# A decoder layer with a gathered expert stage: the on-chip row ring moved to a multiple of 8,192 bytes

## The chip, the cores and the metric

One core of a Trainium2 chip runs the whole kernel. The metric is the device time of one execution, in microseconds: the median of three runs is 3116.35 us (3115.84 to 3116.93). All arithmetic is in float32.

## The reference, cut to what matters

The layer normalises 1,040 tokens (16 meta tokens and 1,024 inputs), projects them, runs differential attention beside a gated causal convolution, projects the two back and adds the residual. Then comes the expert stage, with which this change has to do. For each of 1,024 tokens, and for each of 8 heads, it takes a query, scores it against two sets of 128 keys, keeps the 16 best pairs, and so names 16 of 16,384 experts:

```
q = (xt @ wq).reshape(PEER_CHUNK, PEER_HEADS, 2, PEER_HALF)
s = jnp.einsum('thpk,hpnk->thpn', q, subkeys)
...
e = i1 * PEER_KEYS + i2
gate = jax.nn.softmax(c_top, axis=-1)
act = jax.nn.gelu(jnp.einsum('thkd,td->thk', u_tab[e], xt), approximate=False)
w = (gate * act)
return jnp.einsum('thk,thkd->td', w, v_tab[e])
```

Every token thus needs 128 rows of u and 128 rows of v, each of 1,024 floats. A last norm follows. `x` is (1, 1024, 1024), `peer_u` and `peer_v` are (1, 16384, 1024), `peer_wq` is (1, 1024, 2048).

## The kernel before, in words

The program has two phases, one after the other, each in a block of its own. `mixer_phase` does the norm, the input projection, the convolution and the attention of the first four tiles of 128 tokens. `expert_phase` does the experts of all eight tiles, and beside them the output projection of all tiles and the attention of the last four.

In the expert phase a step is one tile and one head: 64 steps, of 16 experts each, so 1,024 gathers in all. The table in device memory has one row for each expert, u beside v: 2,048 floats, 8,192 bytes. Gather g (`pool.indirect_dma_start`, L1040) brings 128 such rows, one to a partition, and puts them into slot g mod 8 of `ring`, a tensor of 8 slots of 8,192 bytes in each partition. GpSimd issues it when slot g mod 8 is free (`b_free`) and, at the first of a step, when the step's expert numbers are there (`b_route`).

What then happens to gather g, in order: VectorE multiplies the first half of the slot with the normalised tokens `xn_even` or `xn_odd` and sums (`dot`, L1426); ScalarE takes the gelu (L1258), multiplies with the gate (L1184) and makes a diagonal matrix of it (L1191); TensorE multiplies the second half of the slot with this diagonal in 8 matmuls of 64 x 64 x 512 and adds into `acc` (`combine`, L1623). The last of them frees the slot. Between these, written out by hand in the loops over m and k, stand the routing of the steps m + 1 and m + 2 (`queries` at L1597, with weights from `wq_first` for head 0 and `wq_rest` for the others; the top-16 search on VectorE, which uses `top_v`, `top_i`, `cand`, `c_top`, `c_idx`, `c_ab`, `hot` and `pick`), the late attention, the projection and the norms. SyncE issues all other transfers of the phase; they run on the same 16 DMA engines as the gathers.

On-chip memory is given out in the order in which the tensors are named: each begins where the last one ended, its size in a partition rounded up to 32 bytes. The tensors of the mixer phase are given back before those of the expert phase are placed, and the expert phase begins at byte 74,944 of each partition. In the built program of the kernel before, `wq_first` stands at 57,472, `wq_rest` at 75,072, `g2_row` at 132,416, `ring` at 138,560, `xn_even` at 204,096, `xn_odd` at 208,192; in the mixer phase `xT`, which has 8 rows of 4,160 bytes, stands at 81,792.

Of the kernel before, what the change touches and what calls it, by code (L numbers as in the profile page):

```python
# [7 lines left out]
U32 = mybir.dt.uint32  # L8
# [6 lines left out]
P = 128  # L15
D = 1024
# [18 lines left out]
TOPK = 16  # L35
QH = 128
CAND = TOPK * TOPK
RING = 8
# [812 lines left out]
def expert_phase(nc, shared, x, g2, wq, w_out, table, g_final, out, dram):  # L851

    ctx = ExitStack()
    with ctx:
        def sb(name, shape, dt=F32):
            return ctx.enter_context(nc.sbuf_tensor(name, shape, dt))
# [8 lines left out]
        wide, keys_s, wq_first = shared["wide"], shared["keys"], shared["wq0"]  # L865
        mix_t, h_next, proj = shared["mix"], shared["h"], shared["proj"]
        w_out_s = wide[:].rearrange("p (k n) -> p k n", k=KC)
        iota_i = sb("iota_i", [P, TOPK], I32)
        iota_f = sb("iota_f", [P, TOPK])
        wq_rest = sb("wq_rest", [P, PH - 1, KC, 2 * QH])  # L870
        g2_row = sb("g2_row", [P, D])
        gf_half = sb("gf_half", [P, 512])
        ring = sb("ring", [P, RING, 2 * D])
        xn = [sb("xn_even", [P, D]), sb("xn_odd", [P, D])]
        xnT = sb("xnT_cur", [P, KC, P])
        nrm = sb("nrm", [P, 2])
        fin = sb("fin", [P, 2, 2])
        q_s = sb("q_s", [P, 2 * QH])
        qT_s = sb("qT_s", [P, 2, P])
        top_v = sb("top_v", [P, 2, TOPK])  # L880
        top_i = sb("top_i", [P, 2, TOPK], U32)
        cand = sb("cand", [P, CAND])
        cand_t = sb("cand_t", [P, CAND])
        c_top = sb("c_top", [P, TOPK])
        c_idx = sb("c_idx", [P, TOPK], U32)
        c_ab = sb("c_ab", [P, 2, TOPK], U32)
        hot = sb("hot", [P, 2 * TOPK, TOPK])
        pick = sb("pick", [P, 2, TOPK])
        neg_top = sb("neg_top", [P, 1])
        g_exp = sb("g_exp", [P, TOPK])  # L890
        g_sum = sb("g_sum", [P, 2])
        e_row = [sb("e_even", [P, TOPK], U32), sb("e_odd", [P, TOPK], U32)]
        gate = [sb("gate_even", [P, TOPK]), sb("gate_odd", [P, TOPK])]
# [861 lines left out]
def program(nc, x, xt, w_units, w_v, lam_vecs, params, w_out, g2, wq, subkeys_t, table, g_final, out):  # L1755
# [13 lines left out]
    with ExitStack() as ctx:  # L1769

        shared = {
            "wide": ctx.enter_context(nc.sbuf_tensor("wide", [P, KC * D], F32)),
            "keys": ctx.enter_context(nc.sbuf_tensor("keys_s", [P, PH * 2, KEYS], F32)),
            "wq0": ctx.enter_context(nc.sbuf_tensor("wq_first", [P, KC, 2 * QH], F32)),
            "mix": ctx.enter_context(nc.sbuf_tensor("mix_t", [P, KC, P], F32)),
            "h": ctx.enter_context(nc.sbuf_tensor("h_next", [P, D], F32)),
            "ident": ctx.enter_context(nc.sbuf_tensor("ident", [P, P], F32)),
            "pairs": ctx.enter_context(nc.sbuf_tensor("pairs", [P, 2, HP], F32)),
            "sub_gain": ctx.enter_context(nc.sbuf_tensor("sub_gain", [P, 1], F32)),
            "lam": ctx.enter_context(nc.sbuf_tensor("lam_s", [P, 4], F32)),  # L1780
            "proj": [ctx.enter_context(nc.psum_tensor(f"proj{b}", [P, 512], F32)) for b in range(2)],
            "h_in": ctx.enter_context(nc.semaphore("h_in")),
            "w_out_in": ctx.enter_context(nc.semaphore("w_out_in")),
            "keys_in": ctx.enter_context(nc.semaphore("keys_in")),
            "wq0_in": ctx.enter_context(nc.semaphore("wq0_in")),
        }
        mixer_phase(nc, shared, x, xt, w_units, w_v, lam_vecs, params, w_out, wq, subkeys_t, dram)
        expert_phase(nc, shared, x, g2, wq, w_out, table, g_final, out, dram)
# [34 lines left out]
```

## Time and profile before

| | |
|---|---|
| median of three runs | 3116.35 us |
| the profiled execution | 3116.56 us |
| its span, first to last instruction | 3114.8 us |
| mean granted TensorE clock | 0.857 of full speed |
| PE, DVE, ACT, POOL busy | 74%, 67%, 43%, 38% |
| read from device memory, written | 1122.06 MB, 15.28 MB |
| the gathers' queue (q0) | 84.1% of the 16 DMA engines' span |

PE is TensorE, DVE VectorE, ACT ScalarE, POOL GpSimd, SP SyncE, PEld the weight load of TensorE. The busy shares are means over the whole span, and the mixer phase (the first 415 us) looks quite unlike the expert phase. Shares of the DMA engines can go a little over 100%, because the profile lets a packet begin about when the one before it is still ending.

### The profile page before, as it was taken

The page shows a single profiled execution, that of the slowest core. Times are in us where ns is not written, and L with a number is a line of the kernel's source. Part 1 is how long each engine was busy: PE and PEld are TensorE (multiplying, and loading weights), DVE is VectorE, ACT ScalarE, POOL GpSimd, SP SyncE. Part 2 cuts the span into 40 slices and gives each one's busy share as a digit, 9 for nine tenths or more (in the row PEclk, how much of TensorE's full clock was granted, in tenths as well). Part 3 has the DMA queues.
Part 4 walks back from the last instruction along what each step waited for, and adds up shares of the span by engine and source line. Part 5 has one row for each costly group of instructions (what it writes and reads, how often), then busy time and mean ns, then how long its engine had stood idle before and what let it go on. Part 6 is the DMA issues. An engine that isn't in the chain of part 4 may idle for free.

```text
span 3114.8 us, 35490 instructions
## 1 busy us (share of the span) xinstructions
PE 2304.2 (74%) x11776; PEld 846.1 (27%) x11776; DVE 2071.9 (67%) x4903; ACT 1330.3 (43%) x3979; POOL 1176.2 (38%) x1077
## 2 busy tenths in 40 slices
PE   9998847777777777677676777677767777777775
PEld 5555522222222222232222222222222222222111
DVE  2997426666677777777666666666666666666664
ACT  1023514444355555554544444444444444444433
POOL 1001004444444444454444444444444444433442
PEclk9999979898789888999888888978888788887776
DMA  5002139999999999999999999999999999999997
GB/s 213 21 27 72 59 147 420 421 420 421 420 415 410 421 414 411 417 415 419 408 417 421 421 421 421 420 421 416 418 420 417 421 417 419 416 422 418 418 413 312
DMA packets 165608, 1139.68 MB, mean 366 GB/s; under 512 B 18608, under 2 KB 21040, under 8 KB 32688
## 3 DMA queue, kind: packets, MB, share of 16 engines
q0 software_dynamic: 150096, 1082.80, 84.1%
q1 hardware_dynamic: 15328, 54.62, 4.6%
q8 instruction: 93, 1.52, 0.2%
q14 instruction: 91, 0.75, 0.1%
HBM read 1122.06 MB, written 15.28 MB: 365 GB/s over the span
## 4 chain that ended last, share of the span: by engine, by line
DMA 47%; PE 19%; ACT 10%; DVE 6%; issue 4%; POOL 0%; SPq 0%; DVEq 0%; POOLq 0%; ACTq 0%
DMA ring<-table,e_odd 25%; DMA ring<-table,e_even 20%; PE acc L1623 11%; DVE ring L1426 5%; PE qq_ps L1597 4%; ACT diag L1191 2%; ACT weight L1184 2%; ACT L1258 1%; ACT L1177 1%; ACT gelu L1258 1%; PE proj L1570 1%; ACT wide L1215 1%; PE acc L1661 1%; DVE wide L1441 1%; DMA mix_dram<-mix_t 1%
## 5 line engine op out<-in xcount | busy, mean ns | idle before, releaser
L1623 PE MATMUL acc<-ring,diag 64*64 64x512 f32 x8192 | 1330.7, 735 | 729.0 <-ACT diag L1191 704.8
L1426 DVE CUSTOM_DVE_ANT_0 ring<-ring,xn_odd 128x1024 f32<-128x1024 f32 x512 | 626.7, 1224 | 388.4 <-DMA ring<-table,e_odd 191.0
L1040 POOL DMA_INDIRECT ring<-table,e_even x512 | 578.2, 1129 | 797.8 <-PE acc L1623 698.9
L1426 DVE CUSTOM_DVE_ANT_0 ring<-ring,xn_even 128x1024 f32<-128x1024 f32 x512 | 626.8, 1224 | 364.3 <-DMA ring<-table,e_odd 174.7
L1040 POOL DMA_INDIRECT ring<-table,e_odd x512 | 570.5, 1114 | 724.1 <-PE acc L1623 676.3
L1258 ACT ACTIVATE gelu<-dots 128x1 f32<-128x1 f32 x1024 | 205.9, 201 | 1259.0 <-DVE dots L1426 1246.4
L1623 PEld LDWEIGHTS acc<-ring,diag 64*64 64x64 f32 x8192 | 250.5, 150 | 1511.7 <-ACT diag L1191 1338.9
L1191 ACT ACTIVATE diag<-pairs,weight 128x64 f32<-128x64 f32 x1024 | 356.0, 348 | 33.6
L1597 PE MATMUL qq_ps<-wq_rest,xnT_cur 128*128 128x256 f32 x896 | 262.3, 430 | 0.0
L1597 PEld LDWEIGHTS qq_ps<-wq_rest,xnT_cur 128*128 128x128 f32 x896 | 172.3, 208 | 172.9 <-issue 153.0
L1184 ACT ACTIVATE weight<-gelu,gate_even 128x1 f32<-128x1 f32 x512 | 150.7, 294 | 16.7
L1184 ACT ACTIVATE weight<-gelu,gate_odd 128x1 f32<-128x1 f32 x512 | 150.7, 294 | 16.6
L1570 PE MATMUL proj<-wide,mix_t 128*128 128x512 f32 x224 | 142.9, 771 | 6.3 <-DMA mix_t<-mix_dram 6.3
L1258 ACT ACT_TABLE_LOAD x78 | 100.1, 1283 | 1.4
L1426 DVE DVE_READ_ACCUMULATOR2_ANT dots<- 128x1 f32 x1024 | 84.2, 82 | 0.0
L1441 DVE CUSTOM_DVE_ANT_0 wide<-acc,wide 128x328 f32<-128x328 f32 (+4 forms) x72 | 36.8, 548 | 70.5 <-PE acc L1661 70.5
L1177 ACT ACT_TABLE_LOAD x64 | 82.1, 1283 | 1.1
L668 PE MATMUL proj<-xT,w_own 128*128 128x352 f32 x256 | 79.4, 466 | 0.7 <-DVE xT L483 0.7
L504 DVE SCALAR_TENSOR_TENSOR y_even<-u_even,par,y_even 128x1024 f32<-128x1024 f32 x60 | 77.1, 1285 | 2.1
L504 DVE SCALAR_TENSOR_TENSOR y_odd<-u_odd,par,y_odd 128x1024 f32<-128x1024 f32 x60 | 77.1, 1285 | 1.9
L1570 PEld LDWEIGHTS proj<-wide,mix_t 128*128 128x128 f32 x224 | 49.2, 243 | 106.4 <-issue 99.3
L252 POOL COPY mix_t<-yc 128x128 f32<-128x128 f32 x4 | 2.8, 706 | 191.7 <-ACT yc L370 191.7
(237 smaller groups left out, 2098.4 us busy)
## 6 DMA issues: line engine op xcount, KB each, us to landing
ring<-table,e_even POOLq DMA_INDIRECT x512
ring<-table,e_odd POOLq DMA_INDIRECT x512
wq_rest<-wq SPq DMA_DIRECT2D x7, 1024.0 KB, 12.8
w_own<-w_units SPq DMA_DIRECT2D x10, 512.0 KB, 3.7
xT<-xt SPq DMA_DIRECT2D x8, 520.0 KB, 7.4
h_next<-x SPq DMA_DIRECT2D x8, 512.0 KB, 19.4
wide<-w_out SPq DMA_DIRECT2D x2, 2048.0 KB, 8.8
wide<-w_out SPq DMA_DIRECT2D x1, 4096.0 KB, 17.4
```

The costliest lines, as they stand in the source:

```text
L504: dve.scalar_tensor_tensor(out=out[:], in0=u[:, META + k:META + k + SEQ], scalar=cpar[:, c, k:k + 1], in1=out[:], op0=ALU.mult, op1=ALU.ad ...
L668: ins = pe.matmul(banks[n][:, 0:w], w_s[:, k, :], xT[:, k, lo:lo + w], start=(k == 0), stop=(k == KC - 1))
L1040: pool.indirect_dma_start(out=ring[:, g % RING, :], out_offset=None, in_=table[:, :], in_offset=bass.IndirectOffsetOnAxis(ap=e_row[m % 2][ ...
L1177: act.activation(g_exp[:], c_top[:], ACT.Exp, bias=neg_top[:], accum_out=g_sum[:, 0:1]).then_inc(b_gexp, 1)
L1184: act.activation(weight[:, k:k + 1], gelu[:, k:k + 1], ACT.Copy, scale=gate[m % 2][:, k:k + 1]).then_inc(b_weight, 1)
L1191: act.activation(diag[:, g % DIAGS, :], pairs[:, 0, :], ACT.Copy, scale=weight[:, g % TOPK:g % TOPK + 1]).then_inc(b_diag, 1)
L1258: act.activation(gelu[:, k:k + 1], dots[:, k:k + 1], ACT.Gelu).then_inc(b_gelu, 1)
L1426: dve.tensor_tensor_reduce(ring[:, g % RING, 0:D], ring[:, g % RING, 0:D], xn[(m // PH) % 2][:], 1.0, 0.0, ALU.mult, ALU.add, dots[:, k:k ...
L1441: dve.tensor_tensor_reduce(z[:, c, lo_k:hi_k], sc_ps[c][:, 0:hi_k - lo_k], bias[:, off + lo_k:off + hi_k], 1.0, NEG, ALU.add, ALU.max, zma ...
L1570: ins = pe.matmul(proj[b][:], mix_t[:, k, :], w_out_s[:, k, HALF[b]], start=(k == 0), stop=(k == KC - 1))
L1597: ins = pe.matmul(q_ps, xnT[:, k, :], w, start=(k == 0), stop=(k == KC - 1))
L1623: ins = pe.matmul(acc[ACC_OF[t]][ROWS[j], HALF[i]], diag[ROWS[i], g % DIAGS, :], ring[ROWS[i], g % RING, D + j * 512:D + (j + 1) * 512], s ...
```

## The change

The tensors of the expert phase are named in another order. The norm's weight row `g2_row` and nine small tables come ahead of the ring, the query weights `wq_rest` and `gf_half` behind it. No instruction, no size, no wait and no loop is changed.

```diff
         w_out_s = wide[:].rearrange("p (k n) -> p k n", k=KC)
+        g2_row = sb("g2_row", [P, D])
+        hot = sb("hot", [P, 2 * TOPK, TOPK])
         iota_i = sb("iota_i", [P, TOPK], I32)
         iota_f = sb("iota_f", [P, TOPK])
+        top_v = sb("top_v", [P, 2, TOPK])
+        top_i = sb("top_i", [P, 2, TOPK], U32)
+        pick = sb("pick", [P, 2, TOPK])
+        c_top = sb("c_top", [P, TOPK])
+        c_idx = sb("c_idx", [P, TOPK], U32)
+        c_ab = sb("c_ab", [P, 2, TOPK], U32)
+        g_exp = sb("g_exp", [P, TOPK])
+        ring = sb("ring", [P, RING, 2 * D])
         wq_rest = sb("wq_rest", [P, PH - 1, KC, 2 * QH])
-        g2_row = sb("g2_row", [P, D])
         gf_half = sb("gf_half", [P, 512])
-        ring = sb("ring", [P, RING, 2 * D])
         xn = [sb("xn_even", [P, D]), sb("xn_odd", [P, D])]
         xnT = sb("xnT_cur", [P, KC, P])
         nrm = sb("nrm", [P, 2])
         fin = sb("fin", [P, 2, 2])
         q_s = sb("q_s", [P, 2 * QH])
         qT_s = sb("qT_s", [P, 2, P])
-        top_v = sb("top_v", [P, 2, TOPK])
-        top_i = sb("top_i", [P, 2, TOPK], U32)
         cand = sb("cand", [P, CAND])
         cand_t = sb("cand_t", [P, CAND])
-        c_top = sb("c_top", [P, TOPK])
-        c_idx = sb("c_idx", [P, TOPK], U32)
-        c_ab = sb("c_ab", [P, 2, TOPK], U32)
-        hot = sb("hot", [P, 2 * TOPK, TOPK])
-        pick = sb("pick", [P, 2, TOPK])
         neg_top = sb("neg_top", [P, 1])
-        g_exp = sb("g_exp", [P, TOPK])
```

## Rows read from the trace of the kernel before

**Rows 1.** Busy time by stretch, all engines, granted clock, DMA share, rate.
```profile
core 0: us, PE busy (x) PEld busy (x) DVE busy (x) ACT busy (x) POOL busy (x), PEclk, DMA share, GB/s
0.00:440.00 440.00, 381.99 (x1288) 222.31 (x1288) 266.80 (x361) 115.20 (x241) 27.49 (x53) 0.95 0.24 90
...
500.00:900.00 400.00, 294.67 (x1570) 92.86 (x1566) 266.71 (x668) 172.97 (x537) 170.28 (x152) 0.88 1.01 421
900.00:1520.00 620.00, 444.65 (x2742) 170.32 (x2738) 452.17 (x1204) 322.04 (x983) 292.92 (x239) 0.90 1.01 414
...
1490.00:1500.00 10.00, 9.40 (x63) 3.43 (x64) 8.87 (x25) 6.83 (x26) 6.08 (x5) 0.85 0.82 309
```

**Rows 2.** Waits from 480 to 3100: engine and line, waited for, us, times, longest.
```profile
POOL ring L1040 <- PE acc L1623: 1371.3, 834, 10.9
...
DVE ring L1426 <- DMA ring<-table,e_odd: 364.4, 412, 9.3
DVE ring L1426 <- DMA ring<-table,e_even: 352.3, 404, 2.3
```

**Rows 3.** DMA queues from 467 to 3100: packets, MB, share of 16 engines.
```profile
DMA packets 156204, 1097.34 MB, mean 417 GB/s; under 512 B 17423, under 2 KB 19535, under 8 KB 25039
...
q0 software_dynamic: 147238, 1072.16, 98.3%
q1 hardware_dynamic: 8800, 23.15, 2.2%
q8 instruction: 82, 1.34, 0.2%
q14 instruction: 84, 0.69, 0.1%
```

**Rows 4.** DMA queues from 1840 to 1860, a stretch of gathers alone.
```profile
DMA packets 1155, 8.42 MB, mean 421 GB/s; under 512 B 128, under 2 KB 128, under 8 KB 128
...
q0 software_dynamic: 1154, 8.41, 101.1%
q8 instruction: 1, 0.02, 0.3%
```

**Rows 5.** The chain that ended last, from 1840 to 1870.
```profile
1829.46 15.44 DMA ring<-table,e_odd
...
1855.81 13.94 DMA ring<-table,e_odd
```

**Rows 6.** GpSimd's first issues of gathers, and the last transfer issued, in order of time.
```profile
460.50 1.02 POOL L1040 DMA_INDIRECT ring<-table,e_even  x1 [44.96 <-DVE e_even L1412]
...
3110.23 2.39 SPq L1064 DMA_DIRECT2D out<-xn_odd  x4
```

**Rows 7.** Tile `ring`: instructions, ns min/median/max, first and last start.
```profile
L1623 PE MATMUL acc<-ring,diag x8192: 589/640/1113, 468.6 to 3103.7; 64*64 64x512 f32 x200
...
L1426 DVE CUSTOM_DVE_ANT_0 ring<-ring,xn_even x512: 1200/1225/1290, 466.3 to 2777.4; 128x1024 f32<-128x1024 f32 x171
...
L1426 DVE CUSTOM_DVE_ANT_0 ring<-ring,xn_odd x512: 1201/1225/1284, 795.4 to 3100.6; 128x1024 f32<-128x1024 f32 x171
```

**Rows 8.** The query matmuls at L1597: ns min/median/max, first and last start.
```profile
L1597 PE MATMUL qq_ps<-wq_rest,xnT_cur x896: 379/379/795, 451.7 to 2994.9; 128*128 128x256 f32 x180
...
L1597 PE MATMUL qq_ps<-wq_first,xnT_cur x128: 379/379/795, 443.8 to 2711.6; 128*128 128x256 f32 x128
```

**Rows 9.** DMA queues from 1516 to 1526, where 4 MB of `w_out` arrive.
```profile
q0 software_dynamic: 345, 2.52, 60.3%
q1 hardware_dynamic: 65, 1.61, 37.3%
```

**Rows 10.** DMA queues from 4 to 12, mostly the 4,160-byte rows of `xT`.
```profile
DMA packets 891, 3.28 MB, mean 410 GB/s; under 512 B 103, under 2 KB 103, under 8 KB 891
...
q1 hardware_dynamic: 891, 3.28, 100.9%
```

## The prediction

> **What bounds the kernel now.** I read the busy time by stretches first, because the page's shares mix two phases. In the mixer phase the DMA engines are 24% busy and PE is the busiest engine; from 467 us on the DMA share is 1.01 and stays there to the end, at 414 to 421 GB/s, while PE, DVE, ACT and POOL all have time left [rows 1]. Then the waits: DVE waits 364.4 + 352.3 = 717 us for gathered rows, and GpSimd waits 1371 us for TensorE to free a slot [rows 2]. The second looks like a bound by TensorE, and the chain of waits settles it. In a quiet stretch a gather is 13.9 to 15.4 us under way from its issue to its landing [rows 5], though the 16 engines need only about 2.5 us for one: 1,048,576 bytes at 421 GB/s [rows 4] are 2.49 us. So some five gathers stand in the queue at any time, and a slot that is freed sooner only waits longer in that queue. The expert phase runs at the rate of the DMA engines.
>
> How completely? From 467 to 3100 us the four queues have 98.3 + 2.2 + 0.2 + 0.1 = 100.8% of the engines' time [rows 3]; in a stretch of gathers alone they have 101.4% [rows 4], which I take for full. The difference, 0.6% of 2,633 us, is 16 us in which the engines starved; the worst ten microseconds, with a share of 0.82, are around 1490 [rows 1]. Whatever makes TensorE or VectorE faster can give back these 16 us and no more.
>
> **Where the tensors go.** The expert phase starts at byte 74,944. Ahead of the ring now stand `g2_row` 4,096, `hot` 2,048, the two iotas 2 x 64, `top_v`, `top_i` and `pick` 3 x 128, `c_top` and `c_idx` 2 x 64, `c_ab` 128 and `g_exp` 64: 6,976 bytes. 74,944 + 6,976 = 81,920 = 10 x 8,192. So the ring does land where the change says. Before, it stood at 138,560 = 16 x 8,192 + 7,488, which is 541 x 256 + 64: every slot begins 7,488 bytes past a multiple of 8,192, and 64 bytes past a multiple of 256. `wq_rest` goes from 75,072 to 147,456 = 18 x 8,192, and `xn_even` from 204,096 to 206,848.
>
> **The change part by part.** Nothing is issued more, less or elsewhere: the instructions, the semaphores and the order on each queue are the same, SP's and GpSimd's too. So each part is a question of whether an address changes a duration.
>
> *The mixer phase and the head, up to 467 us.* The shared tensors and the mixer's own keep their addresses. The loads of `wq_rest` and `g2_row` go to new places behind the block's end. 0 us.
>
> *The gathers.* In the quiet stretch, gathers take 101.1% of 20 us x 16 engines = 323.5 us of engine time for 8.41 MB [rows 4], which is 1,026 row packets (1,154 less the 128 small ones). That is 315.3 ns a packet, or about 314 ns when 1/8 of a completion packet of some 9 ns is taken off. How much of it can hang on the address? The bulk load of `w_out` moves 1.61 MB in 37.3% of 160 us = 59.7 us, so 27.0 bytes per ns [rows 9]; at that rate 8,192 bytes take 303.4 ns. The fixed part of a row packet is therefore about 11 ns. For the rows of `xT` the same sum gives 100.9% of 128 us = 129.2 us over 891 - 103 = 788 packets, 163.9 ns, less 1.2 for the completions 162.7, against 4,160 / 27.0 = 154.1: a fixed part of 8.6 ns [rows 10]. These rows begin at 81,792 + 4,160 k, so their starts lie 128, 192, 0 and 64 bytes past a multiple of 256, one after the other, where every ring slot lies 64 past one; and they cross multiples of 4,096 at other places. Both fixed parts come out alike to about 2 ns, so I see no share of it that belongs to the place. I take 0 for this part. The bounds: below nothing, the whole fixed part would go. At 16 x 27.0 = 432 GB/s instead of 421 the 1,073.7 MB of rows take 2,485 instead of 2,550 us, a gain of 65 us. Above nothing, the whole phase might move at the rate that it has in its busiest long stretch, 414 GB/s against the mean of 417 [rows 1, 3]: 1,097.34 MB then take 2,651 instead of 2,631 us, a loss of 20 us. Both rows are further off than the quiet stretch against `xT`, hence the 0.
>
> Row first for a rule that speaks against this: the two fixed parts, 11 and 8.6 ns, leave room for some 2 ns of difference at most [rows 4, 10]. The Trainium skill (DMA: Bandwidth & Descriptors, How a descriptor splits into AXI transactions) says that a read is cut into transactions of 256 bytes that start at multiples of 256, so that one that starts off such a multiple also moves the unused bytes below its start. It speaks of reads, and the gathers read whole aligned rows; if it held for the writes too, it would make every row packet shorter after the change.
>
> *VectorE and TensorE on the ring.* The dot takes 1200 to 1290 ns over all 1,024 gathers, with the median at 1225 for `xn_even` as for `xn_odd`, which stand 4,096 bytes apart [rows 7]. The eight slots lie in eight places, one of them across 196,608 = 3 x 65,536, and the spread is 90 ns in all. The query matmuls take 379 ns at the least and in the median with `wq_rest` (1,344 bytes past a multiple of 8,192) as with `wq_first` (128 past one) [rows 8]. So I take 0 for both. What hides an error here is the queue of five gathers: a few hundred ns per gather are covered by some 11 to 13 us of waiting in the queue [rows 5]. At best it gives the 16 us of starving back.
>
> *The small tables.* `hot`, `top_v` and the rest move by multiples of 32 bytes, from high to low addresses. Their instructions are VectorE's and ScalarE's, which have time left, so 0 us.
>
> **The sum.** 467 us up to the full stream of gathers (the first is issued at 460.5), 2,633 us of stream, 14.8 us of tail (the last transfer is issued at 3110.2 [rows 6]) are the span of 3114.8; the execution took 1.8 us more, 3116.56, which is 0.2 above the median of the runs. All changes are 0, so I forecast the median again: **3116.4 us**. Runs of this kernel lie within 0.04%, and I take 0.2%, 6.2 us, as what can be told from no change. Its own range is 3112 to 3121.
>
> **The rivals.**
>
> *1. The write at a multiple of 256 bytes saves its split transaction.* Each packet would save the time of the 64 bytes below its start, 64 / 27.0 = 2.4 ns. Per engine that is 8 packets x 1,024 gathers x 2.4 ns = 19.4 us, all of it on the path, as the DMA engines bound the phase: **3097 us**. This is what the page's rule gives if it holds for writes. For it: the fixed part is greater for row packets than for `xT` by just that much [rows 4, 10]. Against it: the gathers' packets overlap one another in the records, which lengthens each of them on paper without costing time, and the queue of rows is fed by GpSimd and that of `xT` by SyncE, so the 2 ns have other explanations. Chance 0.12.
>
> *2. The readers get faster.* If VectorE and TensorE lost time to slots that begin inside an 8,192-byte block, they would free slots earlier, and the starving would go: at most 16 us, **3100 us**. Against it stand the even durations of the dots. Chance 0.03.
>
> *3. Slower: streams that now start at the same place get in each other's way.* After the change the gathers' writes begin at a multiple of 8,192, and so do the rows of `wq_rest` that TensorE reads. If the memory has parts of that size or a divisor of it, more accesses of one moment meet in one part, and the writes stall. It decides from the point where one packet takes over 0.8 ns longer (0.8 x 8,192 = 6.6 us), as no queue hides a longer packet. Priced with the busy stretch, at 414 GB/s throughout, this is + 20 us: **3136 us**. For it: the rate is lower where TensorE and VectorE work most [rows 1]. Against it: there are more transfers of other queues and moments of starving there, which explain the rate, and the slots stand to each other as they did. Chance 0.07.
>
> *4. The ring is not where the change says.* The sum of the sizes excludes it unless another rounding applies; the time would be 3116.4 all the same, and its small chance is in that of the forecast.
>
> **How the numbers follow.** Forecast 0.78, rival 1 0.12, rival 2 0.03, rival 3 0.07. Faster by over 0.2%: 0.12 + 0.03 and 0.01 from the forecast's own spread, 0.16. Slower: 0.07 and 0.01, 0.08. Within: 0.76. The range goes from 3095, which takes in rivals 1 and 2, to 3136, rival 3's price; outside are the outer bounds of the gathers' part, less 65 us above all.
>
> **What the profile of the changed kernel would show.** If I am right, a quiet stretch of gathers shows 421 GB/s and about 1,154 packets in 20 us again, the dots 1225 ns, the `combine` matmuls 589 and 640, the query matmuls 379, and the two stretches before and after 467 us have the same lengths. Rival 1 would show 424 to 425 GB/s in a quiet stretch with dots as before; rival 2 shorter dots or matmuls, a sum of shares above 100.8% and 421 GB/s in the quiet stretch; rival 3 a lower rate in the quiet stretch too. A different length of the head up to 467 us would prove me wrong on what is untouched.

## The result, and the profile after

The changed kernel takes **3080.2 us** (median of 4 runs, 3078.42 to 3081.18) where the kernel before takes 3116.64 us beside it (3115.84 to 3117.58). The ratio is 0.9882, with a 95% interval of 0.9865 to 0.9899. It is 36.4 us faster, and the forecast of 3116.4 us with its range down to 3095 was wrong. The profiled execution of the changed kernel took 3080.33 us, with a span of 3078.6.

First the busy time by stretches of the changed kernel, with the columns of [rows 1].

```profile
0.00:440.00 440.00, 383.17 (x1288) 222.92 (x1288) 266.59 (x360) 115.13 (x241) 27.40 (x53) 0.95 0.25 90
500.00:900.00 400.00, 300.40 (x1580) 96.41 (x1580) 271.57 (x677) 178.38 (x550) 173.93 (x154) 0.87 1.01 425
900.00:1520.00 620.00, 452.87 (x2768) 172.69 (x2760) 454.66 (x1216) 322.65 (x988) 293.49 (x240) 0.89 1.01 421
```

The mixer phase is as it was, with 1,288 matmuls by 440 us in both. In the expert phase the DMA engines are as busy as before, share 1.01, but move 425 instead of 421 GB/s and 421 instead of 414. They are not fuller; each byte takes them less time.

The DMA queues of the changed kernel from 467 to 3064, which answer to [rows 3]:

```profile
DMA packets 156257, 1097.76 MB, mean 423 GB/s; under 512 B 17424, under 2 KB 19536, under 8 KB 25040
...
q0 software_dynamic: 147291, 1072.59, 98.3%
q1 hardware_dynamic: 8800, 23.15, 2.2%
q8 instruction: 82, 1.34, 0.2%
q14 instruction: 84, 0.69, 0.1%
```

Nearly the same packets and bytes, the same shares, in 2,597 instead of 2,633 us. The four shares add up to 100.8% in both, so the starving of the engines is not what was won. The whole gain lies in this stretch: from the landing of the first gather to that of the last it is 2634.4 us before and 2597.1 after, 37.3 us less. The head is 1.1 us longer (the first gather is issued at 461.6 and not at 460.5); from the issue of the last transfer to the end it is 4.6 us in both.

Now a quiet stretch, from 1700 to 1720, of the kernel before and then of the changed one:

```profile
DMA packets 1154, 8.41 MB, mean 421 GB/s; under 512 B 128, under 2 KB 128, under 8 KB 128
...
q0 software_dynamic: 1153, 8.40, 101.0%
q8 instruction: 1, 0.02, 0.3%
```

```profile
DMA packets 1174, 8.53 MB, mean 426 GB/s; under 512 B 133, under 2 KB 133, under 8 KB 133
...
q0 software_dynamic: 1173, 8.52, 100.9%
q14 instruction: 1, 0.01, 0.1%
```

The same can be seen in VectorE's dots, each of which waits for the landing of its gather. Seven of them in that stretch, first and last, of the kernel before and then of the changed one (start, duration, both in us):

```profile
1700.08 1.23 DVE L1426 CUSTOM_DVE_ANT_0 ring<-ring,xn_odd 128x1024 f32<-128x1024 f32 x1 [0.66 <-DMA ring<-table,e_odd]
...
1715.03 1.23 DVE L1426 CUSTOM_DVE_ANT_0 ring<-ring,xn_odd 128x1024 f32<-128x1024 f32 x1 [0.76 <-DMA ring<-table,e_odd]
```

```profile
1700.46 1.22 DVE L1426 CUSTOM_DVE_ANT_0 ring<-ring,xn_odd 128x1024 f32<-128x1024 f32 x1 [0.76 <-DMA ring<-table,e_odd]
...
1715.20 1.22 DVE L1426 CUSTOM_DVE_ANT_0 ring<-ring,xn_odd 128x1024 f32<-128x1024 f32 x1 [0.91 <-DMA ring<-table,e_even]
```

Six periods are 14.95 us before and 14.74 us after: 2.49 and 2.46 us a gather. The dots themselves did not change, nor did TensorE's matmuls on the ring, nor those on `wq_rest`, which moved too. These answer to [rows 7, 8]:

```profile
L1623 PE MATMUL acc<-ring,diag x8192: 588/640/1114, 469.5 to 3067.5; 64*64 64x512 f32 x200
...
L1426 DVE CUSTOM_DVE_ANT_0 ring<-ring,xn_even x512: 1201/1225/1293, 467.3 to 2745.4; 128x1024 f32<-128x1024 f32 x171
...
L1426 DVE CUSTOM_DVE_ANT_0 ring<-ring,xn_odd x512: 1202/1225/1285, 790.8 to 3064.3; 128x1024 f32<-128x1024 f32 x171
```

```profile
L1597 PE MATMUL qq_ps<-wq_rest,xnT_cur x896: 379/379/795, 452.9 to 2957.9; 128*128 128x256 f32 x180
```

The trace also has every DMA packet with its duration. Of the 131,072 row packets, the kernel before has 19% at 309 ns, 44% at 312 and 17% at 319; the changed one has 99% at 309. If the packets are sorted by their ends and every 128th is taken as a landing, the interval from one gather to the next has a median of 2.486 us before and 2.453 us after. The intervals of the kernels below are read in the same way, over all gathers.

### The profile page after: what moved, and what is told of

The parts are those of the page before. It is cut to its first block, busy times and chain, and to the rows that moved or that the text cites. A ratio compares the mean times of both kernels' runs of the same rounds, so it can differ in the third digit from the quotient of the medians.

```text
span 3078.6 us, 35490 instructions
## 1 busy us (share of the span) xinstructions
PE 2300.7 (75%) x11776; PEld 848.3 (28%) x11776; DVE 2071.3 (67%) x4903; ACT 1328.8 (43%) x3979; POOL 1162.7 (38%) x1077
## 4 chain that ended last, share of the span: by engine, by line
DMA 43%; PE 23%; ACT 10%; DVE 6%; issue 3%; POOL 1%; SPq 0%; DVEq 0%; POOLq 0%; ACTq 0%
DMA ring<-table,e_odd 21%; DMA ring<-table,e_even 20%; PE acc L1623 14%; PE qq_ps L1597 5%; DVE ring L1426 4%; ACT diag L1191 2%; ACT weight L1184 2%; ACT L1258 2%; ACT L1177 1%; PE proj L1570 1%; ACT gelu L1258 1%; ACT wide L1215 1%; PE acc L1661 1%; DVE wide L1441 1%; PE s_ps L1614 1%
## 5 line engine op out<-in xcount | busy, mean ns | idle before, releaser
L1040 POOL DMA_INDIRECT ring<-table,e_even x512 | 567.2, 1108 | 791.2 <-PE acc L1623 700.9
L1597 PE MATMUL qq_ps<-wq_rest,xnT_cur 128*128 128x256 f32 x896 | 262.6, 430 | 0.0
L1597 PEld LDWEIGHTS qq_ps<-wq_rest,xnT_cur 128*128 128x128 f32 x896 | 173.1, 209 | 174.1 <-issue 154.0
```

The costliest lines, as they stand in the source:

```text
L1040: pool.indirect_dma_start(out=ring[:, g % RING, :], out_offset=None, in_=table[:, :], in_offset=bass.IndirectOffsetOnAxis(ap=e_row[m % 2][ ...
L1597: ins = pe.matmul(q_ps, xnT[:, k, :], w, start=(k == 0), stop=(k == KC - 1))
```

## The experiments

The question is which boundary counts, and for whom. Theory A: a DMA write that does not start at a multiple of 256 bytes costs the DMA engine more. Theory B: the ring's place to 8,192 or 4,096 bytes counts, as blocks of the memory. Theory C: the other tensors that moved did it. Theory D: the loss comes from a collision of the writes with the engines' reads.

### The ring alone, four places

Each kernel gets a filler (a tensor that nothing uses) ahead of the ring and one behind it, which sum to 256 or 768 bytes, so that all tensors that follow keep their place modulo 256. The first, on the changed kernel:

```diff
+        ahead = sb("ahead", [P, 16])
         ring = sb("ring", [P, RING, 2 * D])
+        behind = sb("behind", [P, 48])
```

> The changed kernel with the ring alone shifted: 64 bytes ahead of it, 192 behind it, so that the ring starts 64 bytes past a multiple of 8,192 and all that follows keeps its residue modulo 256. Theory A (a write that starts at a multiple of 256 bytes is cheaper): about 3116 us, 421 GB/s in quiet stretches, packets of gathers as before the change. Theory B (the ring's place to 8,192 or 4,096 bytes matters, blocks of memory): also slow or part of the way, 3090 to 3116. Theory C (it is the other moved tensors, wq_rest and the small tables): 3080, 427 GB/s.

The other three are on the kernel before, with `ahead` of 48 floats and `behind` of 16; of 16 and 48; of 176 and 16.

> The kernel before with the ring alone shifted by 192 bytes to 138,752, a multiple of 256 (and 512) but 7,680 past a multiple of 8,192; 64 bytes behind it, so that all that follows keeps its residue modulo 256. Theory A (256): 3080 us and 426 to 427 GB/s, the whole gain. Theory B (4,096 or 8,192): 3116, 421 GB/s. Theory C (other tensors): 3116.

> The kernel before with the ring alone shifted by 64 bytes to 138,624, a multiple of 128 and not of 256; 192 bytes behind it. Theory A with 256: 3116 or, if the cost goes by the bytes between the multiple below and the start, a little slower, 3120 to 3135. Theory A with a finer boundary of 128: 3080. Theories B and C: 3116.

> The kernel before with the ring alone shifted by 704 bytes to 139,264 = 17 x 8,192; 64 bytes behind it; the order of the tensors is that of before, wq_rest and the tables stay. Theory A and theory B: 3080 us, 427 GB/s. Theory C (other tensors): 3116.

Measured, all beside the kernel before at 3117.06 us:

| ring | past a multiple of 256 | of 8,192 | us | ratio (95%) | interval, us |
|---|---|---|---|---|---|
| changed, + 64 | 64 | 64 | 3116.78 | 1.000 (0.999 to 1.001) | 2.486 |
| before, + 192 | 0 | 7,680 | 3083.32 | 0.989 (0.988 to 0.991) | 2.453 |
| before, + 64 | 128 | 7,552 | 3115.44 | 0.999 (0.998 to 1.000) | 2.487 |
| before, + 704 | 0 | 0 | 3082.81 | 0.989 (0.987 to 0.991) | 2.453 |

The first kernel has all of the change but 64 bytes, and all of the gain is gone. The second has the order of the tensors of before and the ring 512 bytes short of a multiple of 8,192, and the gain is there. The second refutes B, and both refute C. The quiet stretch from 1700 to 1720 of the first, then of the second:

```profile
DMA packets 1153, 8.41 MB, mean 420 GB/s; under 512 B 128, under 2 KB 128, under 8 KB 128
...
q0 software_dynamic: 1152, 8.39, 100.9%
```

```profile
DMA packets 1174, 8.54 MB, mean 427 GB/s; under 512 B 131, under 2 KB 131, under 8 KB 131
...
q0 software_dynamic: 1173, 8.54, 101.1%
```

138,752 is a multiple of 512 as well. One more place, 139,008 = 543 x 256 (the kernel before with fillers of 112 and 16 floats), tells 256 from 512:

> The kernel before with the ring alone shifted by 448 bytes to 139,008 = 543 x 256, an odd multiple of 256, so not of 512. A boundary of 256: 3081 to 3083 us, 427 GB/s in quiet stretches. A boundary of 512 or more: 3116 us, 421 GB/s.

It took 3082.01 us beside 3116.38, ratio 0.989 (0.987 to 0.991), interval 2.453 us. The boundary is 256 bytes.

### Gathers alone, eleven places

A program that does nothing but gather, with no reader of the slots (nothing of the layer is computed); only the offset of the slots changes from stage to stage:

```
OFFSETS = [0, 64, 128, 192, 256, 320, 512, 4096, 32, 4064, 0]
for off in OFFSETS:
    for g in range(24):
        pool.wait_ge(landed[n % 8], ...)
        pool.indirect_dma_start(out=space[:, lo:lo + 2 * D], ...)     # lo = off // 4 + (n % 8) * 2 * D
```

> Gathers alone: eleven stages of 24 gathers of 128 rows of 8,192 bytes, eight slots in flight, no engine reads them, nothing else of the layer is computed. The slots start 0, 64, 128, 192, 256, 320, 512, 4096, 32, 4064 and 0 bytes past a multiple of 8,192. Theory A (the write's start modulo 256 decides, by the DMA write alone): 2.453 us a gather at 0, 256, 512 and 4096, about 2.484 at all others, so stages of some 61.5 and 62.2 us with the drain, 427 and 422 GB/s. Theory A' (the boundary is 512): 256 is slow too. Theory D (it takes the reads of VectorE and TensorE beside the writes, a collision): all stages alike at 427.

A stretch of each stage of this program; the columns are start and end, length, POOL busy, granted clock, DMA share, GB/s:

```profile
30.00:70.00 40.00, 9.39 (x10) 1.00 1.01 427
100.00:135.00 35.00, 8.45 (x9) 1.00 1.01 422
165.00:200.00 35.00, 8.45 (x9) 1.00 1.01 422
230.00:265.00 35.00, 8.45 (x9) 1.00 1.01 422
290.00:325.00 35.00, 10.27 (x11) 1.00 1.01 428
360.00:395.00 35.00, 7.51 (x8) 1.00 1.01 422
420.00:455.00 35.00, 9.39 (x10) 1.00 1.01 427
485.00:520.00 35.00, 9.39 (x10) 1.00 1.01 427
552.00:587.00 35.00, 8.45 (x9) 1.00 1.01 421
616.00:651.00 35.00, 8.45 (x9) 1.00 1.01 421
680.00:715.00 35.00, 9.04 (x10) 1.00 1.01 427
```

The rows come in the order of the offsets. At 0, 256, 512 and 4096 it is 427 to 428 GB/s, at all others 421 to 422. (At the start of the first stage the stores to the output still share the engines, 7.4% in its row; the last stage has the same offset without them.) The intervals are 2.453 us on the boundary; 2.484 at 64 past it, 2.479 at 128, 2.484 at 192, 2.486 at 320, and 2.492 at 32 and at 4064 (224 past). Here and in the programs below they are medians of a stage from its sixth interval to the last but one; another choice moves those off the boundary by up to 7 ns. Each of these programs ran once. No engine reads the slots here, so D falls: of the 33 ns that the layer's median interval lost, 31 appear in the DMA write alone.

### Loads by SyncE, and what moves where

> Plain loads by SyncE alone, nothing else of the layer is computed: nine stages of 24 loads of 128 rows, eight in flight. Write start and read start, in bytes past a multiple of 256, and row size: (0,0,8192), (64,0,8192), (128,0,8192), (0,64,8192), (64,64,8192), (256,0,8192), (0,0,4096), (64,0,4096), (0,0,8192). Theory A for writes on any queue: stages 2, 3, 5 and 8 slow by 1.2% (31 ns of 2.45 us for 8,192-byte rows), the others fast. Theory A as the page has it, reads: stages 4 and 5 slow. Theory E (only GpSimd's queue shows it): all alike.

A stretch of the first six stages (columns as above):

```profile
20.00:60.00 40.00, 0.00 (x0) 1.00 1.01 427
90.00:128.00 38.00, 0.00 (x0) 1.00 1.01 422
152.00:190.00 38.00, 0.00 (x0) 1.00 1.01 422
214.00:252.00 38.00, 0.00 (x0) 1.00 1.01 427
276.00:314.00 38.00, 0.00 (x0) 1.00 1.01 421
330.00:380.00 50.00, 0.00 (x0) 1.00 1.01 427
```

The write side decides (stages 2, 3 and 5), and SyncE's queue shows it as GpSimd's does. A read of device memory that starts 64 bytes past the boundary costs nothing (stage 4: 427, interval 2.453 us). For rows of 4,096 bytes the interval goes from 1.248 to 1.279 us. That is 31 ns again for half of the bytes, so the cost is of the packet: 31 / 8 = 3.9 ns for each of the 8 packets that an engine moves.

> Transfers by SyncE alone, nothing of the layer is computed, 24 of a kind: loads of 2,048-byte rows with the write at 0 and 64, loads of 16,384-byte rows at 0 and 64, stores of 8,192-byte rows with (write, read) at (0,0), (0,64), (64,0), then loads of 8,192-byte rows at 64 and at 0. If the cost is one of each packet (31 ns for 8 packets at 8,192 and at 4,096 bytes): 31 ns a transfer more for 2,048 and for 16,384 bytes too. If it goes by the bytes: 8 and 62 ns. For the stores: if it is the write side of the DMA engine, the third kind is slow and the second is not; if it is the on-chip memory, neither or only the second.

| transfer | on the boundary | 64 bytes past it | more |
|---|---|---|---|
| load, 2,048-byte rows | 0.646 us | 0.671 us | 25 ns |
| load, 16,384-byte rows | 4.862 | 4.900 | 38 |
| load, 8,192-byte rows | 2.453 | 2.487 | 34 |
| store, 8,192, read in the on-chip memory | 2.453 | 2.502 | 49 |
| store, 8,192, write in device memory | 2.453 | 2.513 | 60 |

The cost grows by 13 ns where the bytes grow eightfold, so it is nearly one of each packet. The first row is the least firm: on the boundary several intervals of 2,048-byte rows take 0.66 to 0.87 us. The stores gave what was not expected: both their sides are sensitive. That rests on one execution. A stretch of each store stage, (0,0), (0,64), (64,0); an additional zero column is DVE's:

```profile
302.00:352.00 50.00, 0.00 (x0) 0.00 (x0) 1.00 1.01 427
370.00:415.00 45.00, 0.00 (x0) 0.00 (x0) 1.00 1.01 420
432.00:476.00 44.00, 0.00 (x0) 0.00 (x0) 1.00 1.01 417
```

### A forecast from the intervals, and a better version

With 2.492 us at 32 bytes past the boundary the layer's time could be forecast. The changed kernel with `ahead` of 8 floats and `behind` of 56:

> The changed kernel with the ring alone shifted by 32 bytes, 224 bytes behind it. The gathers alone took 2.492 us each at a start 32 bytes past a multiple of 256, 2.484 at 64 and 2.453 at 0. Theory A (the write's start modulo 256 sets the pace of the phase) therefore wants some 900 to 1,000 gathers x 8 ns = 7 to 8 us more than the kernel before: 3124 us (3121 to 3127). A theory in which any place off the boundary costs the same: 3116 to 3117.

3125.53 us beside 3116.24, ratio 1.0031 (1.0019 to 1.0042): slower than the kernel before, by 9.3 us where 7 to 8 were forecast.

The last two: `wide`, `keys_s`, `wq_first`, `mix_t` and `h_next` put at multiples of 256 as well, and the changed kernel once more, on one chip.

```diff
+            "lead": ctx.enter_context(nc.sbuf_tensor("lead", [P, 32], F32)),
             "wide": ctx.enter_context(nc.sbuf_tensor("wide", [P, KC * D], F32)),
...
+        ahead = sb("ahead", [P, 32])
         ring = sb("ring", [P, RING, 2 * D])
```

> The changed kernel with 128 bytes more ahead of the shared tensors and 128 ahead of the ring: now wide, keys_s, wq_first, mix_t and h_next start at multiples of 256 too, and the ring at 82,176 = 321 x 256, no longer at a multiple of 8,192. If every packet off the boundary costs 4 ns, some 3,300 packets of other transfers in the phase are 208 an engine, x 4 ns = 0.8 us: 3079 to 3080, the same as the changed kernel. If the place to 8,192 has a share of its own in the gain of the changed kernel: 3082 to 3084, as where the ring alone was shifted.

> The changed kernel again, beside the others on one chip: 3080 us (3078 to 3082). It shows whether the 2 to 3 us between it (3080.2) and the kernels with the ring alone shifted (3082.0, 3082.8, 3083.3) are the chip's or the kernel's.

3080.63 us (3079.5 to 3083.46) and 3082.26 us (3081.06 to 3082.98), beside 3116.24. They cannot be told apart, so this version is no better than the changed kernel, and no share of the multiple of 8,192 can be seen. The changed kernel's own second measurement moved by 2.1 us; between its first 3080.2 and the kernels with the ring alone on the boundary lie 1.8 to 3.1 us, so most of that is not the place.

## Why the prediction was wrong

**What bounds the kernel: right.** The DMA engines set the phase's time, with share 1.01 in both traces. That is why 31 ns a gather, which no wait and no busy share shows, reached the end undiminished.

**Where the tensors go, and the head, the readers and the small tables at 0: right.** The dots and matmuls kept their durations to the nanosecond in the median, and moving everything else without the ring's last 64 bytes gave 3116.78 us. The head did change, by the 1.1 us that the prediction had named as a sign of an error in what is untouched. That looks like scatter and not like the place: in the ten traces of the layer the first gather is issued between 460.0 and 462.1 us, at 460.0 and 461.7 with the changed order and the ring off the boundary, at 460.3 to 461.6 with it on one.

**The step that failed is the gathers, where I wrote that both fixed parts come out alike to about 2 ns, "so I see no share of it that belongs to the place".** The term of the sum was 0; the runs show some 33 us less. In the loads alone a packet on the boundary takes 4.862 / 8 us at 16,384 bytes and 2.453 / 8 at 8,192, which leaves 5.5 ns that do not grow with the bytes; 64 bytes past the boundary 3.9 ns come on top. Four things were wrong with that comparison:

- A difference of 2 ns was taken for none. Over the 8,192 packets of an engine 2 ns are 16 us, and the 2.4 ns between 11 and 8.6 are rival 1's 19.4 us, where the forecast's own range allowed for 6.2.
- By its address none of its members was a clean write on the boundary. The ring stood 64 past a multiple of 256, `wide`, into which the bulk load goes, 128 past one, and three in four rows of `xT` lay off it. Agreement of such rows could not show that the place costs nothing.
- The loads of `xT` are at the start of the program. In the loads alone at 64 past, the intervals run, in ns:

```
2467 2453 2453 2453 2461 2484 2482 2490 2482 2484 ...
```

So five intervals are at full pace or near it, some 12 us, and only then the cost shows. My stretch of `xT` ended at 12 us. Its rows did run at full pace: 976 of the 1,024 packets took 161 ns, as did all 640 of that size in the expert phase of the changed kernel, where the kernel before has a mean of 163.2. The fast start thus hid the cost of `xT`'s own place, and the 2.4 ns that I put aside compared a row that paid with one that did not yet pay.
- The durations of packets overlap in the records (a share of 101%), so a difference of a few ns can't be read from two shares of different kinds of stretch. The same stretch of another kernel can be compared, as above.

**Rival 1 named the mechanism and mis-sized it.** I gave it 0.12 and 3097 us. The Trainium skill (DMA: Bandwidth & Descriptors, How a descriptor splits into AXI transactions) has the 256-byte boundary right, but tells it of reads and by the unused bytes below the start. Here the start of the read in device memory costs nothing, and 64, 192 and 320 bytes cost the same 31 to 33 ns a gather. I priced 64 bytes at 27 bytes per ns, 2.4 ns a packet. That the cost is alike at 64, 192 and 320 bytes speaks against a price by these bytes; what in the DMA engine makes it is not shown. Measured are 3.9 ns in the gathers alone, which makes 8 x 1,024 x 3.9 = 32 us instead of 19.4. With its right size the rival gives 3116.6 - 32 = 3085 us. In the layer the median interval fell by 33 ns, and 1,023 intervals make 33.8 us. The comparisons gave 36.4 and 34.0. What the gathers take above 1,023 median intervals (transfers of other queues between them, and starving) is 91.2 us before and 87.7 after, and 89 to 93 us in the other eight traces of the layer, wherever the ring stands. So the last 3 us are about what this part moves anyway. The packets of other queues have a small share in it: before, 54% of the 2,560 packets of 4,096 bytes in the phase took 159 ns, after 99.6%, though `h_next` and `mix_t` still stand 128 past the boundary. At 3.9 ns for each of some 5,600 packets of 2,048 bytes and more, 350 an engine, it is 1.4 us at most. That they had been held up behind the gathers' packets is argued and not shown.

**The other rivals** fell: the readers did not get faster, and rows that start with the slots at a multiple of 8,192 got in nobody's way. The outer bound of the gathers' part, less 65 us, held.

The range failed by the same error. It went down to the price of rival 1 and not to a bound of its unknown, so a mechanism right in kind fell 15 us outside.

## What to carry to other kernels

Where the DMA engines are the bound, put each destination of the repeated loads and gathers on a multiple of 256 bytes in the partition; a filler of at most 224 bytes does it, and the larger boundary brings nothing more. The gain is some 4 ns a packet on each engine (3 at 2,048 bytes, 5 at 16,384), so count packets, not bytes: it is 1.2% here at 8,192 bytes and was 2.5% at 4,096 in the loads alone. When a trace is to tell whether a place matters, first ask whether it holds one example on the good side, and take it in steady state, not in the first 15 us of a burst. And before a difference is called nothing, multiply it by the number of packets.

## What the runs showed of the hardware

- A write of rows from device memory into the on-chip memory that starts off a multiple of 256 bytes costs about 31 ns per 128 packets of 8,192 bytes (3.9 ns a packet and engine) at 64, 128, 192 and 320 bytes, and 39 ns at 32 and at 224 past a multiple; at 0, 256, 512 and 4,096 it costs nothing. Both GpSimd's and SyncE's queue show it, GpSimd's at all these places, SyncE's at 0, 64, 128 and 256.
- In loads and gathers 64 bytes past the boundary the cost appears only after some five or six transfers of 1 MB in an unbroken stream, and after four of 2 MB (rows of 16,384 bytes). After a pause the packets take 309 ns again. In stores whose read was off the boundary it was there from the first interval, 2.507 us. That a buffer between the read and the write side fills up in that time would explain it, and also why packets of other queues are held up; this is argued and not shown.
- A read of device memory off the boundary costs nothing in loads. In stores, a read of the on-chip memory 64 bytes past it cost 49 ns and a write into device memory 60 ns per 1 MB, in one execution.
